# Recurrent steps of an encoder layer: turning the keys by transposing matmuls

## The chip, the cores and the metric

The kernel runs on one core of one Trainium2 chip. The metric is device time in microseconds (us), the median of several runs; less is better. Engines are named as in the profile: PE is TensorE's matmul side, PEld its weight loads, DVE is VectorE, ACT is ScalarE, POOL is GpSimd, SP is SyncE, whose queue issues the transfers.

## The reference, cut to what matters

One encoder layer with two branches, for a sequence of 1024 tokens and one of 256. The branch that the change touches is a recurrence over tokens, run forward and backward, for 16 heads of width 64:

```python
def step(S, inp):
    r_t, w_t, kh_t, ak_t, v_t, kt_t = inp
    sk = jnp.einsum('bhvk,bhk->bhv', S, kh_t)
    S = S * w_t[:, :, None, :] - sk[..., None] * ak_t[:, :, None, :] + v_t[..., None] * kt_t[:, :, None, :]
    return S, jnp.einsum('bhvk,bhk->bhv', S, r_t)
S0 = jnp.zeros((B, H, N, N), jnp.float32)
_, o = lax.scan(step, S0, (r, w, kh, ak, v, kt), reverse=reverse)
```

The rest of the layer (projections, grouped attention, gates, output projection, a feed-forward of width 4096, layer norms) is not touched. Everything is float32.

## The kernel before, in words

The kernel is a row of stages, each with its own program for every engine and a barrier behind it. The names of PSUM and SBUF tiles carry the stage: `at_` attention, `ra_` the scaled inputs, `rg_` gates, `rc_` the recurrence (the function `state_stage`), `mg_` the merge, `tl_` the tail. The order of the work on each engine is written out by hand; engines meet by semaphores.

`state_stage` does the recurrence in chunks of 64 tokens (`CH`): 40 steps `g`, 20 chunks for each of two groups of heads. A step has 8 units `u` (four pairs of heads, forward and backward), and in each unit the two heads lie on partitions 0 to 63 and 64 to 127. For unit `u`, `ub[g % 3]` holds blocks of 64 columns: values (column 0), two blocks of keys (`CH:3*CH`), two blocks of queries (`3*CH:5*CH`), and at `5*CH:6*CH` a 64x64 identity, which is written once and stays.

Scores are made by `scores(g, q)`, q = 0 to 3, two units a call, so four matmuls a call (two units by two heads). The keys are the stationary operand (64 rows, 128 columns), and 192 columns stream by: 128 of queries, which give the scores, and the 64 of the identity, which give the keys turned round. DVE multiplies the first 128 columns by a mask into `SC` (`mask`, L1738), ACT copies the last 64 into `KT` (`transposes`, L1692), once DVE's mask of the same call is done. Both wait for the one semaphore `sc_ready`, which the last matmul of the call raises.

Within step g, PE's order is: `scores(g+1,0)`; 32x32 corner matmuls (L1629), which I call X; state times queries (L1640) with the values of the next step between (L1593); `scores(g+1,1)`; two kinds of 64x64 matmuls (L1654, L1657); corner matmuls L1665; `scores(g+1,2)`; the matmuls of `Bs` by `NF` (L1601), which I call U; `scores(g+1,3)`; the state update with `KT` (L1601), K; the outputs (L1601), C. A float32 matmul stands in the trace as two weight loads and two matmul records; a transposing one, as those of the gate stage (L1165), as one of each.

SP's queue loads the units of step g+3 one at a time, each released by a point in PE's program.

Of the kernel before, what the change touches and what calls it, by code (L numbers as in the profile page):

```python
# [17 lines left out]
CH = 64  # L18
# [1456 lines left out]
def state_stage(nc, hbm, cst, pv, oR, ring, ahead, pool, ub_ready, xT, oa_ready, late):  # L1475

    with Stage(nc, "rc") as st:
# [11 lines left out]
        ps = st.psum()  # L1489
        BB, UB, OB, CB = 0, 1, 2, 3  # L1490
        ALTERNATE = (0, 4, 1, 5, 2, 6, 3, 7)
        ident64, centre = cst[:, C_ID64:C_ID64 + CH], cst[:, C_CEN:C_CEN + CH]
# [78 lines left out]
        def _(pe):  # L1571
            def scores(g, q):

                x = ub[g % 3]
                if q == 0:
                    pe.wait_ge(ub_ready[g % 3], 16 * U * (g // 3 + 1))
                    if g == 2:
                        pe.wait_ge(id_done, 1)
                n = 4 * g + q
                if n >= 2:  # L1580
                    pe.wait_ge(masked, n - 1)
                    pe.wait_ge(kt_done, n - 1)
                for j in range(2):
                    for h in range(2):
                        rows = slice(64 * h, 64 * h + 64)
                        last = pe.matmul(ps[:, 4 + 2 * (q % 2) + h, 192 * j:192 * j + 192], x[rows, 2 * q + j, CH:3 * CH],  # L1586
                                         x[rows, 2 * q + j, 3 * CH:6 * CH], start=True, stop=True)
                last.then_inc(sc_ready, 1)

            def values(g, u):  # L1590
# [14 lines left out]
            def half(h):  # L1605
                return slice(64 * h, 64 * h + 64)

            def other(h):
                return slice(64 - 64 * h, 128 - 64 * h)

            pe.wait_ge(set_up, 1)
            for q in range(4):
                scores(0, q)
            for u in range(U):
                values(0, u)
            for g in range(NSTEP):
                x, sc, v = ub[g % 3], SC[g % 2], X[g % 2]
                if g + 1 < NSTEP:
                    scores(g + 1, 0)
# [5 lines left out]
                for u in ALTERNATE:  # L1625
                    for h in range(2):
                        d = u // 4
                        i, o = (64 * h, 64 * h + 32) if d == 0 else (64 * h + 32, 64 * h)
                        last = pe.matmul(ps[o:o + 32, CB, 32 * u:32 * u + 32], sc[i:i + 32, u, h, o % 64:o % 64 + 32],  # L1629
                                         r_[d][i:i + 32, u % 4, :], start=True, stop=True)  # L1630
# [7 lines left out]
                for u in range(U):  # L1638
                    for h in range(2):
                        last = pe.matmul(ps[half(h), BB, CH * u:CH * u + CH], x[half(h), u, 3 * CH:4 * CH], S[half(h), u, :],  # L1640
                                         start=u == 0, stop=True, skip_group_check=True)
# [4 lines left out]
                if g + 1 < NSTEP:  # L1646
                    scores(g + 1, 1)
# [4 lines left out]
                for u in range(U):  # L1652
                    for h in range(2):
                        pe.matmul(ps[half(h), OB, CH * u:CH * u + CH], S[half(h), u, :], x[half(h), u, 4 * CH:5 * CH],  # L1654
                                  start=u == 0, stop=True, skip_group_check=True)
                    for h in range(2):
                        last = pe.matmul(ps[half(h), BB, CH * u:CH * u + CH], sc[other(h), u, h, 0:CH], v[other(h), u, h, :],  # L1657
                                         start=False, stop=True, skip_group_check=True)
                last.then_inc(b_ready, 1)
                pe.wait_ge(w_done, g + 1)  # L1660
                for u in ALTERNATE:
                    for h in range(2):
                        d = u // 4
                        i, o = (64 * h + 32, 64 * h) if d == 0 else (64 * h, 64 * h + 32)
                        last = pe.matmul(ps[o:o + 32, CB, 256 + 32 * u:256 + 32 * u + 32], Wt[i:i + 32, u, :],  # L1665
                                         n_[d][i:i + 32, u % 4, :], start=True, stop=True)
# [1245 lines left out]
```

## Time and profile before

| | |
|---|---|
| time, median of 3 runs | 3261.92 us (3259.46 to 3267.58) |
| the profiled execution's own time | 3262.58 us |
| its span, first to last instruction | 3260.4 us |
| PE busy | 3132.7 us, 96% of the span |
| DVE, ACT, POOL busy | 59%, 32%, 12% |
| PE and PEld records | 26248 each |
| granted TensorE clock, mean | 0.990 of full |

Busy shares are means over stages. A wait is put down to what came last by the profile; "issue" is idle time in which the engine waited for nothing that the profile shows.

### The profile page before, as it was taken

How to read it: one execution, taken by the hardware profiler on the slowest of the kernel's cores; microseconds unless marked ns; L12 is line 12 of the kernel's file. 1: busy time of each engine (PE TensorE's matmuls, PEld its weight loads, DVE VectorE, ACT ScalarE, POOL GpSimd, SP SyncE). 2: the span in 40 equal slices, each digit the busy share in tenths (PEclk: the TensorE clock that was granted, in tenths of full speed). 3: DMA queues.
4: the chain of work that ended last, by engine and by line, in shares of the span. 5: the costliest groups of instructions: out<-in, count | busy, mean ns of one | idle time of the engine just before them, and what ended most of it. 6: DMA issues, size and time to landing. Idle time of an engine off the chain costs nothing. (4 is left out here: it accounts for less than half of the span.)

```text
span 3260.4 us, 61273 instructions
## 1 busy us (share of the span) xinstructions
PE 3132.7 (96%) x26248; PEld 2098.7 (64%) x26248; DVE 1919.9 (59%) x3037; ACT 1055.9 (32%) x1731; POOL 387.1 (12%) x250
## 2 busy tenths in 40 slices
PE   9999999999999988989999999999999999999997
PEld 4565665545555556777787777667666666666665
DVE  2337762667776699546566565645555456545446
ACT  2327662334333225533443441003311111221111
POOL 0000000000000363300000233324200000300002
PEclk9999999999999999999999999999999999999998
DMA  3222101334453512455565423312122122122121
GB/s 142 58 55 53 46 32 51 118 125 141 153 173 123 209 65 90 160 180 163 165 173 153 173 92 126 140 65 72 59 65 79 63 65 78 59 97 83 60 65 65
DMA packets 225979, 336.98 MB, mean 103 GB/s; under 512 B 56112, under 2 KB 184496, under 8 KB 218672
## 3 DMA queue, kind: packets, MB, share of 16 engines
q1 hardware_dynamic: 225712, 333.08, 31.6%
q8 instruction: 209, 3.42, 0.4%
q14 instruction: 58, 0.48, 0.0%
HBM read 230.13 MB, written 96.34 MB: 100 GB/s over the span
## 5 line engine op out<-in xcount | busy, mean ns | idle before, releaser
L656 PE MATMUL ra_ps<-xT,ring 128*128 128x512 f32 (+1 forms) x1152 | 429.8, 526 | 0.0
L2415 PE MATMUL tl_ps<-merged,pool 128*128 128x320 f32 x1440 | 405.7, 434 | 2.7 <-PEq L108 2.1
L2415 PEld LDWEIGHTS tl_ps<-merged,pool 128*128 128x128 f32 x1440 | 273.9, 191 | 119.2 <-issue 5.2
L656 PEld LDWEIGHTS ra_ps<-xT,ring 128*128 128x128 f32 x1152 | 214.3, 190 | 199.0 <-issue 189.3
L2678 DVE TENSOR_TENSOR oR<-tl_ps,oR 128x320 f32<-128x320 f32 x416 | 202.0, 489 | 151.2 <-PE tl_ps L2415 148.5
L2500 ACT ACTIVATE ring<-tl_ps 128x320 f32<-128x320 f32 x96 | 42.0, 437 | 533.8 <-PE tl_ps L2415 533.8
L2415 PE MATMUL tl_ps<-hold,pool 128*128 128x320 f32 x720 | 202.6, 432 | 0.0
L2684 DVE TENSOR_TENSOR merged<-tl_ps,ring 128x320 f32<-128x320 f32 x96 | 47.2, 491 | 255.5 <-PE tl_ps L2415 140.4
L2415 PE MATMUL tl_ps<-xT,pool 128*128 128x320 f32 x640 | 182.7, 432 | 0.0
L2415 PEld LDWEIGHTS tl_ps<-hold,pool 128*128 128x128 f32 x720 | 136.8, 190 | 57.0
L2415 PE MATMUL tl_ps<-merged,sums 128*128 128x320 f32 x544 | 160.7, 435 | 5.8 <-DVE oR L2676 3.2
L317 PE MATMUL at_ps<-xT,ring 128*128 128x512 f32 (+1 forms) x432 | 159.1, 521 | 0.0
L1586 PE MATMUL rc_ps<-pool 64*128 64x192 f32 x1280 | 151.3, 354 | 7.2 <-DVE rc_ps L1787 3.9
L2415 PEld LDWEIGHTS tl_ps<-xT,pool 128*128 128x128 f32 x640 | 121.6, 190 | 50.7
L1738 DVE TENSOR_TENSOR rc_SC<-rc_ps,cst 128x512 f32<-128x512 f32 x160 | 110.2, 689 | 71.9 <-PE rc_ps L1586 71.9
L342 PE MATMUL at_ps<-at_qk 128*128 128x512 f32 (+1 forms) x288 | 129.1, 585 | 8.8 <-ACT at_p L410 8.3
L2415 PEld LDWEIGHTS tl_ps<-merged,sums 128*128 128x128 f32 x544 | 102.0, 190 | 53.8 <-issue 12.9
L354 PE MATMUL at_ps<-at_turned,at_v 32*128 32x256 f32 x2176 | 129.5, 381 | 4.5 <-DVE at_ot L494 4.1
L354 PEld LDWEIGHTS at_ps<-at_turned,at_v 32*128 32x128 f32 x2176 | 111.3, 185 | 32.4 <-issue 26.4
L317 PEld LDWEIGHTS at_ps<-xT,ring 128*128 128x128 f32 x432 | 82.1, 190 | 72.6 <-issue 68.9
L471 DVE TENSOR_REDUCE at_mx<-at_ps 128x1 f32<-128x1024 f32 (+1 forms) x80 | 84.2, 1052 | 60.8 <-PE at_ps L342 60.7
L2415 PE MATMUL tl_ps<-hold,sums 128*128 128x320 f32 x432 | 119.2, 432 | 0.0
(334 smaller groups left out, 5454.7 us busy)
## 6 DMA issues: line engine op xcount, KB each, us to landing
pool<-ub SPq DMA_DIRECT2D x320, 160.0 KB, 2.8
ub<-ra_ub SPq DMA_DIRECT2D x32, 1280.0 KB, 5.4
pool<-in_w_ff SPq DMA_DIRECT2D x32, 1024.0 KB, 4.8
pool<-in_w_ff SPq DMA_DIRECT2D x64, 512.0 KB, 3.5
ring<-in_w_in SPq DMA_DIRECT2D x38, 512.0 KB, 3.7
pool<-in_w_merge SPq DMA_DIRECT2D x15, 1024.0 KB, 4.9
ub<-ra_v SPq DMA_DIRECT2D x16, 640.0 KB, 6.4
xT<-in_xT SPq DMA_DIRECT2D x15, 640.0 KB, 6.9
```

Of the source, the lines that this page charges most:

```text
L317: last = pe.matmul(ps[:, z_bank(i) + j, 0:n], w[:, i % 3, 128 * k:128 * k + 128], xT[:, k, t0:t0 + n], start=(k == 0), stop=(k == KT - 1))
L342: last = pe.matmul(ps[:, 2 * (t % 2) + b // 512, 0:n], qk[:, h, t0:t0 + 128], qk[:, QH + h // (QH // KVH), k0 + b:k0 + b + n], start=True, ...
L354: last = pe.matmul(ps[:, 4 + i, 0:256], values_of(g, i, j), pT[g % 2][32 * i:32 * i + 32, j].rearrange("p t q -> p (t q)"), start=(j == 0) ...
L471: dve.reduce_max(mx[:, c:c + 1], scores_of(t), AX.X).then_inc(mx_done, 1)
L656: last = pe.matmul(ps[:, bank + j, 0:n], w[c][:, 128 * i:128 * i + 128], xT[:, i, t0:t0 + n], start=(i == 0), stop=(i == KT - 1))
L1586: last = pe.matmul(ps[:, 4 + 2 * (q % 2) + h, 192 * j:192 * j + 192], x[rows, 2 * q + j, CH:3 * CH], x[rows, 2 * q + j, 3 * CH:6 * CH], st ...
L1738: dve.tensor_tensor(SC[g % 2][:, 2 * q:2 * q + 2, :, :], score_view(ps, q, 0, 2 * CH), cst[:, at:at + 128].unsqueeze(1).unsqueeze(1).broad ...
L2415: last = pe.matmul(bank(n, b), lhs(k), rhs(k), start=(fresh and k == 0), stop=(k == d - 1), skip_group_check=True)
L2500: act.activation(cp[n % 2][:, c, :], bank(n, b), ACT.Copy).then_inc(done, 1)
L2678: dve.tensor_tensor(y, bank(n, b), y, ALU.add).then_inc(done, 1)
L2684: dve.tensor_tensor(hidden(n, i, j), bank(n, b), cp[n % 2][:, c, :], ALU.add).then_inc(done, 1)
```

## The change

The identity columns leave the matmuls of the scores. Each call of `scores` now first makes the scores of its four pairs of unit and head with 128 streamed columns, and then turns the keys of the same four by `pe.transpose`: keys as the stationary operand again, and the constant identity `ident64` streamed, into the PSUM columns where the turned keys stood before. `sc_ready` is raised by the last transposing matmul. What DVE and ACT do is the same, and the identity is still written into `ub`.

```diff
                 for j in range(2):
                     for h in range(2):
                         rows = slice(64 * h, 64 * h + 64)
-                        last = pe.matmul(ps[:, 4 + 2 * (q % 2) + h, 192 * j:192 * j + 192], x[rows, 2 * q + j, CH:3 * CH],
-                                         x[rows, 2 * q + j, 3 * CH:6 * CH], start=True, stop=True)
+                        pe.matmul(ps[:, 4 + 2 * (q % 2) + h, 192 * j:192 * j + 128], x[rows, 2 * q + j, CH:3 * CH],
+                                  x[rows, 2 * q + j, 3 * CH:5 * CH], start=True, stop=True)
+                for j in range(2):
+                    for h in range(2):
+                        rows = slice(64 * h, 64 * h + 64)
+                        last = pe.transpose(ps[:, 4 + 2 * (q % 2) + h, 192 * j + 128:192 * j + 192], x[rows, 2 * q + j, CH:3 * CH],
+                                            ident64[rows])
                 last.then_inc(sc_ready, 1)
```

On PE, from the corner matmuls L1665 of one step to the corner matmuls L1629 of the next, the order before is this (line, output and inputs, size, count):

```order
L1665 MATMUL rc_ps<-rc_nb,rc_Wt 32x32 x16
L1586 MATMUL rc_ps<-pool 128x192 x4
L1601 MATMUL rc_ps<-rc_Bs,rc_NF 64x64 x16
L1586 MATMUL rc_ps<-pool 128x192 x4
L1601 MATMUL rc_ps<-rc_X,rc_KT 64x64 x16
L1601 MATMUL rc_ps<-rc_SC,rc_X 64x64 x16
L1586 MATMUL rc_ps<-pool 128x192 x4
```

In the changed kernel the same stretch of PE's program (its lines are five further down) is this:

```order
L1670 MATMUL rc_ps<-rc_nb,rc_Wt 32x32 x16
L1586 MATMUL rc_ps<-pool 128x128 x4
L1591 MATMUL rc_ps<-cst,pool 128x64 x4
L1606 MATMUL rc_ps<-rc_Bs,rc_NF 64x64 x16
L1586 MATMUL rc_ps<-pool 128x128 x4
L1591 MATMUL rc_ps<-cst,pool 128x64 x4
L1606 MATMUL rc_ps<-rc_X,rc_KT 64x64 x16
L1606 MATMUL rc_ps<-rc_SC,rc_X 64x64 x16
L1586 MATMUL rc_ps<-pool 128x128 x4
L1591 MATMUL rc_ps<-cst,pool 128x64 x4
```

Nothing has moved; behind every call's four matmuls, now a third narrower, stand four more. The rows of the other engines stand as they did.

## Rows read from the trace of the kernel before

**Rows 1.** The page: transfers of instructions by queue (packets, MB, share of 16 engines).

```profile
q8 instruction: 209, 3.42, 0.4%
```

**Rows 2.** Groups of the recurrence, 1408 to 1840 us (count | busy us, mean ns | idle before).

```profile
L1586 PE MATMUL rc_ps<-pool 64*128 64x192 f32 x1268 | 149.6, 353 | 3.4 <-issue 3.3
L1738 DVE TENSOR_TENSOR rc_SC<-rc_ps,cst 128x512 f32<-128x512 f32 x159 | 109.5, 689 | 71.1 <-PE rc_ps L1586 71.1
L1692 ACT ACTIVATE rc_KT<-rc_ps 128x256 f32<-128x256 f32 x160 | 61.3, 383 | 148.9 <-DVE rc_SC L1738 148.9
...
L1697 ACT ACTIVATE rc_X<-rc_ps 64x512 f32<-64x512 f32 x80 | 47.0, 588 | 6.8 <-PE rc_ps L1593 5.2
...
L1801 DVE TENSOR_SCALAR rc_X<-rc_ps 64x512 f32<-64x512 f32 x40 | 27.8, 695 | 26.1 <-PE rc_ps L1601 26.1
L1772 DVE TENSOR_TENSOR rc_S<-rc_t,pv 128x256 f32<-128x256 f32 x72 | 27.4, 421 | 1.2
L1765 DVE TENSOR_TENSOR rc_t<-rc_ps,rc_S 128x512 f32<-128x512 f32 x36 | 24.9, 691 | 15.2 <-PE rc_ps L1601 15.2
...
L1716 ACT ACTIVATE rc_Bs<-rc_ps 128x512 f32<-128x512 f32 x40 | 23.9, 597 | 14.6 <-PE rc_ps L1657 14.4
...
L1747 DVE TENSOR_SCALAR rc_NF<-rc_nb,cst 128x128 f32<-128x128 f32 x80 | 18.9, 277 | 0.3 <-DMA rc_rb<-rb 0.3
...
L1785 DVE TENSOR_TENSOR oR<-rc_ps,oR 128x256 f32<-128x256 f32 x40 | 15.0, 416 | 0.7 <-PE rc_ps L1601 0.7
```

**Rows 3.** Busy time of the whole recurrence (window, PE, PEld, DVE, ACT, POOL, clock, DMA).

```profile
1407.90:1839.50 431.60, 394.59 (x12672) 336.47 (x12672) 256.38 (x559) 168.41 (x360) 0.17 (x1) 0.99 0.56 158
```

**Rows 4.** Timeline of 1500 to 1504.3 us (start, length, engine, line).

```profile
1500.07 0.63 PEld L1586 LDWEIGHTS rc_ps<-pool 64*128 64x128 f32 x8
1500.07 0.92 PE L1586 MATMUL rc_ps<-pool 64*128 64x192 f32 x8
...
1500.92 1.01 PEld L1601 LDWEIGHTS rc_ps<-rc_X,rc_KT 128*64 128x64 f32 x32 [0.23 <-DVE rc_X L1801]
...
1502.94 0.63 PEld L1586 LDWEIGHTS rc_ps<-pool 64*128 64x128 f32 x8
...
1503.79 0.34 PEld L1629 LDWEIGHTS rc_ps<-rc_rb,rc_SC 32*32 32x32 f32 x32 [0.23 <-issue]
```

**Rows 5.** Timeline of transposing matmuls in the gate stage, in two windows.

```profile
1361.61 0.72 PE L1165 MATMUL rg_ps<-cst,rg_inv 80*128 80x80 f32 x8
...
1300.17 0.98 PE L1165 MATMUL rg_ps<-cst,rg_inv 120*128 120x120 f32 x8
```

**Rows 6.** Timeline of 1507.8 to 1513.1 us.

```profile
1508.22 0.63 PEld L1586 LDWEIGHTS rc_ps<-pool 64*128 64x128 f32 x8
...
1508.37 0.61 DVE L1755 SCALAR_TENSOR_TENSOR rc_NF<-rc_nb,cst,rc_ps 128x128 f32<-128x128 f32 x2 [0.81 <-PE rc_ps L1665]
1509.09 0.34 PEld L1601 LDWEIGHTS rc_ps<-rc_Bs,rc_NF 64*64 64x64 f32 x8 [0.25 <-issue]
...
1510.53 0.78 PEld L1601 LDWEIGHTS rc_ps<-rc_Bs,rc_NF 64*64 64x64 f32 x24 [1.10 <-issue]
```

**Rows 7.** Waits of PE in the recurrence (line, total us, times, longest).

```profile
PE rc_ps L1665 <- issue: 11.7, 8, 2.0
PE rc_ps L1657 <- issue: 7.6, 8, 1.6
...
PE rc_ps L1593 <- issue: 0.8, 1, 0.8
```

**Rows 8.** Windows from the end of one such wait to the end of the next.

```profile
1505.62:1510.53 4.91, 3.94 (x126) 3.16 (x126) 1.99 (x4) 2.60 (x6) 0.00 (x0) 1.00 0.66 188
...
1548.33:1553.14 4.81, 2.90 (x127) 2.43 (x127) 0.69 (x1) 2.16 (x4) 0.00 (x0) 1.00 0.58 159
```

**Rows 9.** Transfers of instructions in the recurrence, 1407.9 to 1839.5 us.

```profile
q8 instruction: 100, 1.64, 1.6%
```

**Rows 10.** Two windows of the gate stage, before and in transposing matmuls.

```profile
1207.00:1218.70 11.70, 4.35 (x17) 2.73 (x15) 11.15 (x18) 1.67 (x4) 1.47 (x1) 0.80 0.36 120
1218.90:1220.20 1.30, 1.30 (x8) 1.30 (x9) 1.30 (x1) 0.37 (x1) 0.00 (x0) 0.50 0.04 13
```

## The prediction

> **What bounds the kernel now.** I read the page first. The change touches one stage, so the next view is the busy time of that stage alone: 431.6 us for 40 steps, 10.8 us a step, with PE busy for 394.6 us and DVE and ACT for 256.4 and 168.4 [rows 3]. PE is the engine to look at, and the reader is to see that it still lacks 37 us. The list of its waits says where: almost all of it is "issue", idle time that no semaphore explains. There are seven such lines with 38 waits and 33.3 us together (11.7 for the first, 0.8 for the last), single ones up to 2.0 us [rows 7]. PE's last matmul runs on for some 0.2 us when the queue is already dry, so PE's program stood still for about 33.3 + 38 x 0.2 = 41 us.
>
> The timeline shows such a wait in the middle of one row of like matmuls: 8 weight loads of U from 1509.09, then nothing for 1.10 us, then the other 24 [rows 6]. Counting between the ends of two such waits gives the cause. From 1505.62 to 1510.53 there are 126 loads and 126 matmuls, and from 1548.33 to 1553.14 there are 127 of each, with quite different work inside [rows 8]: a fixed number of instructions, about 253. The transfers of instructions tell the same. The page has 209 on the queue q8 with 3.42 MB [rows 1], 16.4 KB each, which over 2 x 26248 records is 65 bytes a record; the recurrence has 100 of them [rows 9] for 2 x 12672 records [rows 3], one per 253. So PE's program arrives in pieces of some 253 records, a piece is used up in 4.3 us on average (431.6 / 100), and 38 times in 100 the next one is late. In this stage PE is bound partly by its work and partly by the arrival of its program.
>
> **The change, part by part.** A call before is 8 matmul records in 4 pairs, the two heads of a pair side by side. Its first load starts at 1500.07 and the loads of the next work at 1500.92, 0.85 us later; the same from 1502.94 to 1503.79 [rows 4]. Its matmuls span 0.92 us, and the records are at least 0.32 us long, so with a first load of some 0.11 the four pairs follow at (0.92 - 0.32 - 0.11) / 3 = 0.16 us, for 192 columns.
>
> *Removed: 64 of 192 columns.* A third of 0.16 is 0.054, for four pairs 0.215 us a call. The weight load of 128 columns then has 0.11 us to hide in instead of 0.16; the stage's loads do that now for the 64-column forms (32 loads in 1.01 us, 0.06 a pair, row of 1500.92 in [rows 4]), and I take 0.11 for a pair.
>
> *Added: four transposing matmuls, one record each.* The gate stage has such records at 80 columns, 8 in 0.72 us, and at 120, 8 in 0.98 [rows 5]. With lengths of about 0.23 and 0.27 for the last, they follow at 0.070 and 0.102 us, about 0.8 ns a column; 64 columns are 0.055. All those span 80 or 120 rows, and none shows two halves of the array side by side. Bounds: two by two, 0.11 us a call; one behind the other, 0.22. The regular halves run side by side, so I take the first. A call then gives back 0.215 - 0.11 = 0.10 us of PE, 16 us over 160 calls; by the upper bound, nothing.
> The Trainium skill, "TensorE: Matmul & The Clock Gate", section Terms, has a transpose mode that is four times faster for FP32. By it the 64 columns would cost a quarter of 0.107, 0.03 a pair, and PE's saving would be 0.16 a call and 25 us in all; the gate stage's records, at twice that time, speak against it, and the sum goes by them.
>
> *What of it reaches the end.* Two of the four calls of a step have a cover. After `scores(g+1,2)`, U needs `NF`, which DVE has at 1508.37 + 0.61 = 1508.98, when the call has just run out (loads until 1508.85) and U starts at 1509.09 [rows 6]. After `scores(g+1,3)`, K waits for DVE's L1801 (the mark on the row of 1500.92 [rows 4]). Shorter calls there lengthen those waits. That leaves two calls, 0.2 us a step, 8 us at most. A second loop bounds it further: from U's end L1801 (0.70), K (1.01), L1765 (0.69), L1772 twice (27.4 / 36 = 0.76), the outputs twice (0.75), L1747 twice (0.47), the mask L1738 (0.69), ACT's L1692 (0.38), L1697 twice (1.18), L1692 again (0.38), L1716 (0.60) and U itself (about 0.95) are 8.6 us [rows 2, 4], and twelve handovers of 0.03 to 0.2 us make it 9.3 or more. A step without its share of the 41 us is (431.6 - 41) / 40 = 9.8 with the ends of the stage in it. The loop holds one mask of a first call, so 0.1 a step at most comes through it. I take -1 us, between 0 and -8, near the loop's end of it.
>
> *Added: records.* A call has 8 loads and 8 matmuls now and will have 8 + 4 of each: 8 records more, 1280 in 160 calls, 5.05% of 25344, five pieces more. The time from one piece to the next when PE waits is set by the transfer, not by what PE did; what changes is the work that a piece holds. Work is 431.6 - 41 = 390.6 us, 3.91 us a piece, then 390.6 / 105 = 3.72. Each late piece is met 0.19 us earlier. 38 waits become 38 x 1.05 = 40 and their mean goes from 1.08 to 1.27: 50.8 us against 41, +10. Of the 62 pieces that were in time, those less than 0.19 us ahead become late. Lateness runs over 2 us for 38 pieces, some 19 per us, and it is denser near zero; with the 62 spread over one us, 12 become late by 0.1: +1. A saving of work also comes back 40% as waiting. And the five more joints have their share of bad luck, up to 5 x 4.3 = 21.5 us if no piece had slack. I take +13 for all of it, somewhat over the bare +11.
>
> **Sum:** -1 + 13 = +12 us on the profiled execution's 3262.6, 3274.6. The median of the runs is 0.7 below that execution, so 3274. A measurement can tell about 0.3%, 10 us.
>
> **Rivals.** (a) *The arrival of the program sets the whole pace.* Then 105 pieces at 4.3 us: +21 us, 3284. For it: 38 waits in 100, and the time from piece to piece where PE waited is 4.91 and 4.81 us [rows 8], longer than the mean. Against it: 62 pieces without a wait. (b) *The shorter calls make up for it.* All 8 us of the uncovered calls arrive while waits grow by 10: -4 to +5, 3263. It needs DVE's and ACT's loop to be slacker than its sum. (c) *Faster.* The masks wait for calls, 71.1 us in all [rows 2], and each call ends 0.10 us earlier, so the loop shortens at all four calls: 0.4 a step, -16 us, against which the pieces are late less than thought, because they are asked for earlier too; it decides if the growth of the waits stays under 6 us. 3252. The Trainium skill, "Perfetto Trace Analysis", section Transposes, asks for a transpose instead of a standard matmul wherever one is logically meant; that speaks for this side, and no run here shows it yet. (d) *Transposing costs more than its columns.* One behind the other, with a gap for the change of mode, or a lower clock: clock 0.50 stands over eight transposing matmuls of the gate stage [rows 10]. But PE had been busy for only 4.35 of the 11.7 us before, and at 1300.17 the same form runs at the full rate [rows 5]. With 0.1 us more a call +16 on top, 3290. The Trainium skill, "TensorE: Matmul & The Clock Gate", Part 4, says that transpose mode does not count as PE being busy for the clock; the gate stage doesn't settle it, as PE was idle there anyway.
>
> **How the numbers follow.** The forecast, +6 to +18 us: 0.55. (a) 0.13, (b) 0.20, (c) 0.06, (d) 0.06. The range of eight in ten leaves out the lower edge with (c) and the upper with (d): 3260 to 3288. The forecast's own range is 3268 to 3281. Slower by over 0.3%: three quarters of the forecast with (a) and (d), 0.41 + 0.13 + 0.06 = 0.60. Within 0.3%: the rest of the forecast and (b), 0.34. Faster: 0.06.
>
> **What the profile of the changed kernel would show.** The queue q8 has 214 packets, 105 in the recurrence. PE has 26888 records. A call's loads and matmuls reach the next work in 0.75 us instead of 0.85; if it is still 0.85, the transposing records ran one behind the other. Busy time of PE in the stage falls by up to 16 us while its "issue" waits grow from 33 to 45 us or more, in some 50 places. The waits of U and K for DVE grow by about 0.1 us each. I am wrong if the issue waits don't grow (the pieces then were not what PE waited for), or if the stage gets shorter than 425 us.

## The result, and the profile after

The changed kernel takes 3288.07 us (median of 4 runs, 3285.79 to 3289.22), the kernel before 3264.75 us (4 runs). The ratio is 1.0069, 95% interval 1.0055 to 1.0083: slower by 22.5 us, between 18 and 27. The forecast was slower by 12 us, 3274; 12 lies below the interval.

The profiled execution has a span of 3284.9 us, 24.5 more than before. The page's row for the transfers of instructions answers to [rows 1]: five more on q8.

```profile
PE 3140.4 (96%) x26888; PEld 2123.3 (65%) x26888; DVE 1919.3 (58%) x3037; ACT 1057.1 (32%) x1731; POOL 387.0 (12%) x250
...
q8 instruction: 214, 3.51, 0.5%
```

PE has 26888 matmul records, 640 more, and as many more loads. Windows of the changed kernel, in the recurrence and behind it (window, PE, PEld, DVE, ACT, POOL, clock, DMA), beside [rows 3]:

```profile
1409.10:1861.40 452.30, 396.46 (x13312) 358.33 (x13312) 256.18 (x556) 169.16 (x360) 0.10 (x1) 0.96 0.54 151
1861.40:3284.90 1423.50, 1388.78 (x5102) 969.18 (x5100) 779.00 (x1406) 300.34 (x542) 243.12 (x149) 0.99 0.25 84
```

For the kernel before, a window set to the recurrence alone and one to what follows it:

```profile
1408.00:1838.70 430.70, 394.55 (x12672) 336.45 (x12672) 255.67 (x556) 168.41 (x360) 0.07 (x1) 0.99 0.56 159
1838.70:3260.40 1421.70, 1386.94 (x5102) 967.98 (x5100) 778.18 (x1406) 300.23 (x542) 242.97 (x149) 0.99 0.25 84
```

The recurrence grew by 452.3 - 430.7 = 21.6 us, what follows by 1.8, and what stands ahead by 1.1. DVE and ACT did the same work in it to within 1 us.

One call in the timeline of the changed kernel answers to [rows 4]:

```profile
1506.84 0.52 PEld L1586 LDWEIGHTS rc_ps<-pool 64*128 64x128 f32 x8
1506.84 0.71 PE L1586 MATMUL rc_ps<-pool 64*128 64x128 f32 x8
...
1507.28 0.25 PEld L1591 LDWEIGHTS rc_ps<-cst,pool 64*128 64x128 f32 x4
1507.39 0.28 PE L1591 MATMUL rc_ps<-cst,pool 64*128 64x64 f32 x4
...
1507.60 0.34 PEld L1634 LDWEIGHTS rc_ps<-rc_rb,rc_SC 32*32 32x32 f32 x32
```

From the first load at 1506.84 to the loads of the corner matmuls at 1507.60 it is 0.76 us, against 0.85 before. The transposing matmuls cost what was forecast: four take 0.28 us with a last one of 0.22, so the two pairs follow at 0.06, and the two halves of the array work side by side. The change thus spares PE 0.09 us a call, some 14 us over 160 calls. None of it reaches the end, and PE's busy time in the stage didn't fall either: it is 396.5 us after 394.6. PE's waits for its program answer to [rows 7]; these are the largest of the kind in the recurrence:

```profile
PE rc_ps L1670 <- issue: 18.1, 13, 2.0
PE rc_ps L1606 <- issue: 10.8, 15, 1.4
PE rc_ps L1659 <- issue: 10.0, 11, 1.4
PE rc_ps L1662 <- issue: 5.3, 7, 1.3
```

With five smaller lines (11 waits, 5.4 us) they are 57 waits with 49.6 us now, 38 with 33.3 before. With 0.2 us each for the matmul that still ran, PE's program stood still for 61 us instead of 41: +20, nearly the whole 21.6. The distance between the ends of such waits is again nearly the same number of records, 128 matmuls and 128 loads here for one piece, and 251 and 252 for two (beside [rows 8]):

```profile
1588.79:1593.01 4.22, 3.22 (x128) 2.89 (x128) 1.35 (x4) 1.45 (x4) 0.00 (x0) 1.00 0.65 180
...
1513.14:1521.78 8.64, 8.28 (x251) 7.48 (x252) 6.30 (x14) 2.98 (x7) 0.00 (x0) 1.00 0.49 138
```

And q8 brought 105 pieces during the recurrence, where [rows 9] has 100:

```profile
q8 instruction: 105, 1.72, 1.7%
```

The packet times in the two traces tie the waits to these transfers directly. Before the change the start of PE's next matmul or load comes over 0.6 us behind the last one 35 times in the recurrence, and 34 of these gaps end 1.1 to 1.7 us after a transfer on q8 has landed; after the change 50 of 52 do. The transfers start 4.23 us apart on average before and 4.22 after, and don't overlap: each takes 1.1 us, and the next starts 2.3 us or more after its end.

### The profile page after: what moved, and what is told of

Read it like the earlier page. It is cut to its first block and busy times, and to the rows that moved or that the text cites. A ratio compares the mean times of both kernels' runs of the same rounds, so it can differ in the third digit from the quotient of the medians.

```text
span 3284.9 us, 62553 instructions
## 1 busy us (share of the span) xinstructions
PE 3140.4 (96%) x26888; PEld 2123.3 (65%) x26888; DVE 1919.3 (58%) x3037; ACT 1057.1 (32%) x1731; POOL 387.0 (12%) x250
## 5 line engine op out<-in xcount | busy, mean ns | idle before, releaser
L1586 PE MATMUL rc_ps<-pool 64*128 64x128 f32 x1280 | 119.4, 306 | 4.5 <-DVE rc_ps L1792 3.9
```

The lines of the kernel that those rows point to most:

```text
L1586: pe.matmul(ps[:, 4 + 2 * (q % 2) + h, 192 * j:192 * j + 128], x[rows, 2 * q + j, CH:3 * CH], x[rows, 2 * q + j, 3 * CH:5 * CH], start=Tru ...
```

## The experiments

Theory A is that of the prediction: the recurrence pays for the pieces in which PE's program arrives, so for records, whatever they do. Theory B is that the transposing matmuls, or PE's work, set the time. Theory A follows the size of the measured loss, so its ranges are mostly higher than the +13 of the forecast. All times are against the kernel before on the same chip; a ratio is turned into us by 3263.

**Records alone.** Eight of the sixteen corner matmuls of a step are made twice, which gives the change's number of records without touching the scores.

```diff
-                for u in ALTERNATE:
+                for u in (*ALTERNATE[:4], *ALTERNATE):
                     for h in range(2):
                         d = u // 4
```

> The kernel before, with 8 of the 16 corner matmuls L1629 of each step made twice (the first result is overwritten by the same one), so 32 more records a step, as many as the change adds, and no transposing matmul. The 64 records of this line take 0.38 us a step, so 32 more are some 0.19 us of PE, 7.6 us over 40 steps. Theory A, the arrival of the program: 105 pieces instead of 100, waits for it grow as in the changed kernel, the time +18 to +28 us. Theory B, the transposing matmuls themselves (their clock or their place) cost the time: +0 to +8 us.

Measured: ratio 1.0053 (1.0035 to 1.0070), +17 us (11 to 23). The recurrence has the change's records:

```profile
1406.80:1855.50 448.70, 403.04 (x13312) 344.68 (x13312) 255.87 (x557) 169.34 (x360) 0.15 (x1) 0.99 0.53 153
```

Most of the loss is there without one transposing matmul, and it is well over this kernel's 8 us of added work. The value is just under theory A's range, and its interval reaches into it.

**Twice as many.** The same with all sixteen (`(*ALTERNATE, *ALTERNATE)`).

> The kernel before with all 16 corner matmuls L1629 of each step made twice, 64 more records a step and 0.38 us more of PE, 15 us in all. Theory A: 110 pieces at 4.3 us or a little less, twice the loss of the run with 8, +36 to +50 us. Theory B: no more than the work, +0 to +15 us.

Measured: ratio 1.0089 (1.0066 to 1.0112), +29 us (22 to 37). The recurrence took 467.1 us for 110 pieces, in an execution 9 us above the median. The loss is more than the work, so theory B falls here too, but it is less than twice the loss with eight, and below the range I gave theory A but for the end of its interval.

**Narrow scores, nothing turned.** No record is added, and some 34 us of PE's work, by the estimate of the prediction, are taken away. DVE sets the PSUM banks to zero once, ahead of the steps; `KT` is zero and the state lacks its updates.

```diff
-                        last = pe.matmul(ps[:, 4 + 2 * (q % 2) + h, 192 * j:192 * j + 192], x[rows, 2 * q + j, CH:3 * CH],
-                                         x[rows, 2 * q + j, 3 * CH:6 * CH], start=True, stop=True)
+                        last = pe.matmul(ps[:, 4 + 2 * (q % 2) + h, 192 * j:192 * j + 128], x[rows, 2 * q + j, CH:3 * CH],
+                                         x[rows, 2 * q + j, 3 * CH:5 * CH], start=True, stop=True)
```

> The kernel before with 128 streamed columns instead of 192 in the scores and no turning of keys at all: ACT copies zeros into KT, so the state is not updated by them. Records stay as they are, PE's work falls by 0.215 us a call, 34 us in all. If the loop through DVE and ACT and the arrival of the program bound the stage (theory A), little of it arrives: 0 to -8 us, with issue waits that grow. If PE's own work bounds it (theory B): -20 to -34 us.

Measured: ratio 1.0000 (0.9988 to 1.0012), nothing, within 4 us. The profiled execution's recurrence is 6 us shorter:

```profile
1410.00:1834.80 424.80, 373.02 (x12672) 327.33 (x12672) 256.11 (x557) 166.93 (x360) 0.00 (x0) 0.97 0.55 160
```

This is the sharpest of the runs. A third of the scores' streaming is worth at most a few us. PE's busy time fell by 21.5 us and not by 34; the granted clock of 0.97 and 12 more waits, each with the end of a matmul that counts as busy, account for part of the difference. PE's waits for the program grew from 33.3 to 37.8 us, in 50 places. Zeroing the banks costs about 2 us once: at the start of the stage PE waits 6.0 us for DVE instead of 3.9. PE is busy for 394.6 of 431.6 us in [rows 3], and still its work isn't the bound.

**Both together.** Narrow scores, nothing turned, and eight corner matmuls twice: the change's records with less work than the change.

> The kernel before with 128 streamed columns and no turning of keys (ACT copies zeros into KT), and 8 of the 16 corner matmuls L1629 made twice: the changed kernel's number of records and its narrow scores, without one transposing matmul. PE's work is 34 us less than before, plus 7.6 us for the doubled matmuls. Theory A, a price per record through the arrival of the program, about 0.018 us each in the runs so far: +17 to +24 us, as the changed kernel. Theory B, transposing matmuls cost part of it: clearly less, +0 to +12 us.

Measured: ratio 1.0073 (1.0058 to 1.0088), +24 us (19 to 29), the change's own loss, at the upper end of theory A's range and over all of theory B's.

```profile
1408.90:1859.60 450.70, 383.20 (x13312) 337.36 (x13312) 256.03 (x557) 168.52 (x360) 0.00 (x0) 0.97 0.53 151
```

No transposing matmul is in this kernel. What separates it from the narrow one is 32 records a step, with an estimated 7.6 us of work in all.

**Records taken away.** Half of the output matmuls of each step are left out, in the kernel before and in the changed one; part of the outputs is missing.

```diff
-                heads(ps, OB, lambda u, h: v[:, u, h, :], lambda u, h: sc[:, u, h, CH:2 * CH], False).then_inc(o_ready, 1)
+                heads(ps, OB, lambda u, h: v[:, u, h, :], lambda u, h: sc[:, u, h, CH:2 * CH], False, (1, 3, 5, 7)).then_inc(o_ready, 1)
```

> The kernel before with 8 of the 16 output matmuls C left out in each step (odd units; part of the outputs is missing), 32 records fewer a step. PE's work falls by 0.23 us a step, 9 us in all, as much as 32 records always carry. Theory A: 95 pieces, the time falls by 15 to 22 us. Theory B: by no more than the work, 0 to -9 us.

> The changed kernel with the same 8 output matmuls of each step left out (part of the outputs is missing), so it has as many records as the kernel before. Theory A: within 4 us of the kernel before, and 17 to 24 us above the run with these matmuls left out of the kernel before. Theory B: still 14 us or more above the kernel before.

Measured: without them the kernel before is at 0.9948 (0.9932 to 0.9965), -17 us (-22 to -11). The changed kernel without them is at 0.9994 (0.9983 to 1.0004), -2 us, in effect the kernel before, whose number of records it has:

```profile
1407.30:1835.30 428.00, 377.69 (x12672) 339.71 (x12672) 255.76 (x556) 166.00 (x360) 0.13 (x1) 0.96 0.55 160
```

Each is in theory A's range; the two lie 15 us apart, where theory A had 17 to 24. Theory B's +14 is excluded.

**Where it ends.** Fourteen of the sixteen left out (`(7,)` in place of `(1, 3, 5, 7)`), 91 pieces.

> The kernel before with 14 of the 16 output matmuls C of each step left out (most of the outputs is missing), 56 records fewer a step, 91 pieces instead of 100. PE's work falls by 0.4 us a step, 16 us in all. Theory A with 4.3 us for every piece: -35 to -38 us. Theory A with a second bound, the loop through DVE and ACT of 9.3 us a step: less than in proportion to the run with 8 left out, -20 to -32 us. Theory B: -5 to -16 us, its work.

Measured: ratio 0.9938 (0.9921 to 0.9954), -20 us (-26 to -15). Taking away 24 records a step more than in the run before gave 3 us more, and the intervals overlap. With 4.3 us for every piece it should have been -35 to -38; with a second bound I had expected -20 to -32, and the value is at the near end of that.

```profile
1407.20:1810.90 403.70, 364.77 (x11552) 306.25 (x11552) 255.33 (x556) 164.38 (x360) 0.10 (x1) 0.98 0.59 169
```

So at about 10 us a step something besides the program holds PE up. Its waits say what, in part:

```profile
PE rc_ps L1640 <- DVE rc_S L1772: 12.6, 36, 1.1
```

Before, this wait was there once, with 0.3 us. PE now waits 36 times for DVE's L1772 to finish the state, while 23.9 us of waits for the program are left. L1772 is a member of the prediction's loop through DVE and ACT, which it put at 9.3 us or more; that the rest of this loop is what makes L1772 late was argued, not shown.

**Half of the change.** The change in two of the four calls, once where DVE's work covers the calls and once where it doesn't (`if q >= 2:` and `if q < 2:` around the new form, the old one in the `else`).

> The change made in the calls 2 and 3 of each step alone, whose shorter time is hidden behind DVE's L1755 and L1801. 16 records more a step, 102 to 103 pieces. Theory A: half of the change's loss, +8 to +13 us. Theory B, the shorter calls matter and only covered ones are lost: more than half of the loss, +14 us or more, here, and about none in the calls 0 and 1.

> The change made in the calls 0 and 1 of each step alone, which no wait for DVE follows, so that 0.1 us of each can arrive, 8 us at most. 16 records more a step. Theory A with the loop as the bound: +8 to +13 us, as in the calls 2 and 3. If saved PE time arrives here: 0 to +5 us.

Measured: covered calls 1.0026 (1.0016 to 1.0037), +8.5 us; uncovered 1.0017 (1.0007 to 1.0027), +5.5 us. Each has 103 pieces. Half of the records give somewhat less than half of the loss. The covered calls are in theory A's range. The uncovered ones miss it, and are close to what I had expected if saved time arrives there; whether they let some of their 0.09 us through stays open, as the intervals of the two overlap (5 to 12 us and 2 to 9).

**Traffic.** The kernel before with four more loads a step into a tile that nobody reads; PE's program is unchanged. This is the first of the four:

```diff
+                    after(sp, dumped[0], 16 * g)
+                    load_unit(sp, hbm, dump, g + 3, 0, dumped[0])
```

> The kernel before with half as much traffic again in the recurrence: the loads of the units 0, 2, 4 and 6 are each followed by another of the same size into a tile that nobody reads. PE's program is the same. If the price of a piece of program lies partly in its transfer standing behind the data's (share of the transfer engines 0.56 now), the pieces take longer and the stage grows by 0.2 us or more a piece, +15 to +50 us. If it is a fixed delay of the fetch: within 5 us.

Measured: ratio 1.0046 (1.0031 to 1.0061), +15 us (10 to 20), in the range for pieces that stand behind data, at its lower end.

```profile
1411.80:1854.90 443.10, 397.76 (x12672) 338.42 (x12672) 256.07 (x557) 168.38 (x360) 0.19 (x1) 0.99 0.70 209
```

It has the same records as in [rows 3] and nearly the same busy times, traffic of 209 GB/s instead of 158, and 12.4 us more than the 430.7 for the same 100 pieces, 0.12 us each. The packet times agree: a piece's own transfer takes 1.1 us as before, but the time from its end to the start of the next grew from 3.12 to 3.25 us. That fits pieces that queue with the data. That the units' own loads came late instead was not excluded by a run, though PE has no wait for a transfer in the recurrence, before or here.

**Two variants for their own sake.** The first turns the keys of both heads of a unit by one transposing matmul over all 128 rows: 20 records a call. Against the changed kernel, with the new places in PSUM and what reads them left out here:

```diff
                 for j in range(2):
-                    for h in range(2):
-                        rows = slice(64 * h, 64 * h + 64)
-                        last = pe.transpose(ps[:, 4 + 2 * (q % 2) + h, 192 * j + 128:192 * j + 192], x[rows, 2 * q + j, CH:3 * CH],
-                                            ident64[rows])
+                    last = pe.transpose(ps[:, 4 + 2 * (q % 2) + j, 256:384], x[:, 2 * q + j, CH:3 * CH], cst[:, C_ID:C_ID + 128])
```

> The changed kernel, but the keys of both heads of a unit are turned by one transposing matmul over all 128 rows, two a call instead of four. Records: 20 a call, against 16 before and 24 in the change, so 102 to 103 pieces. PE's work in a call grows, since the array goes from halves to the whole. Theory A, a price per record: +8 to +12 us against before, half of the change's loss. Theory B, the transposing form costs: as the change, +18 us or more.

Measured: ratio 1.0037 (1.0023 to 1.0050), +12 us (8 to 16), as theory A had it. It is better than the change and worse than before. The call costs PE more:

```profile
1505.77 0.52 PEld L1586 LDWEIGHTS rc_ps<-pool 64*128 64x128 f32 x8
...
1506.41 0.20 PEld L1589 LDWEIGHTS rc_ps<-cst,pool 128*128 128x128 f32 x2
...
1506.78 0.34 PEld L1631 LDWEIGHTS rc_ps<-rc_rb,rc_SC 32*32 32x32 f32 x32 [0.17 <-issue]
```

That is 1.01 us, 0.16 more than before, 26 us in all; PE's busy time in the recurrence is 418 us, 23 more. Yet the recurrence took only 439.2 us, 8.5 more, and PE's waits for its program shrank to 19.0 us in 33 places. Most of the added work went into time that PE had stood still before. So the waits alone don't measure the price: what grew with the 103 pieces is the time for all of them, 4.26 us each.

The second keeps the kernel before and moves the loads of the attention outputs behind those of the units (`range(8 * (g - 36), 8 * (g - 36) + 8) if g >= 36` in place of one at each g from 2 to 33).

> The kernel before, with the 32 loads of attention outputs (160 KB each) moved from the steps 2 to 33 to the last four steps, where the units' loads have ended. Half as much traffic again cost 15 us, so a tenth less in 32 steps would give back about 3 us by the arrival of the program: -1 to -5 us. It could lose where the merge then waits for these loads: up to +10 us.

Measured: ratio 1.0010 (1.0000 to 1.0021), +3 us (0 to 7). The recurrence took 429.3 us in the profiled execution, against 430.7. The expected gain of 1 to 5 us didn't come: moving this traffic, a tenth of the whole by the expectation, to the end brought nothing. No run with more than half of the outputs computed beat the kernel before.

## Why the prediction was right, and where its size was off

**The bound.** "In this stage PE is bound partly by its work and partly by the arrival of its program" named the right mechanism with too much weight on the work. The narrow run takes a third of the scores' streaming away and gains nothing that can be told. The profiled executions side by side show how little the work counts (times in us, of the recurrence):

| kernel | pieces | PE busy, per piece | recurrence, per piece |
|---|---|---|---|
| before | 100 | 3.95 | 4.31 |
| the change | 105 | 3.78 | 4.31 |
| eight corner matmuls twice | 105 | 3.84 | 4.27 |
| sixteen twice | 110 | 3.77 | 4.25 |
| narrow scores | 100 | 3.73 | 4.25 |
| narrow scores, eight twice | 105 | 3.65 | 4.29 |
| half of the outputs | 95 | 3.99 | 4.34 |
| the change, half of the outputs | 100 | 3.78 | 4.28 |
| the change in the covered calls | 103 | 3.84 | 4.29 |
| the change in the uncovered calls | 103 | 3.80 | 4.23 |
| 128-row transposing matmuls | 103 | 4.06 | 4.26 |
| attention outputs loaded late | 100 | 3.95 | 4.29 |
| an eighth of the outputs | 91 | 4.01 | 4.44 |
| more traffic | 100 | 3.98 | 4.43 |

PE's busy time per piece varies by 11%. The time per piece varies by under 3%, but for the two last: one has the other wait, and one has the added traffic. What sets these 4.3 us, of which a transfer itself takes 1.1, stays open.

**The price of the transposing form.** Forecast 0.10 us a call given back, records side by side at 0.055 us; measured 0.09 and 0.06. The estimate by the Trainium skill, "TensorE: Matmul & The Clock Gate", section Terms, 0.03 a pair, is off by a factor of two. Rival (d), a higher cost or a lower clock, fell as the cause of the loss. The transposing matmuls run side by side. The granted clock did fall, from 0.99 in the recurrence to 0.96 (the engine was at the lower of its two levels, 1.2 GHz, for some 32 us of it instead of 10), but it is 0.96 as well in the changed kernel with half of its outputs, which is as fast as before, and 0.99 in the run with eight matmuls doubled, which lost 17 us. By my estimate the lower clock is also why PE's busy time didn't fall by the forecast "up to 16 us": 22 us more at half the rate are some 11 us of work done later, and 19 more waits leave some 4 us of matmuls that run on, which together make up for the 14 that the calls give back.

**What of it reaches the end.** Forecast -1 us between 0 and -8. The narrow run has twice the saving per call and 0 us (within 4), in agreement. With it rivals (b) and (c) fell, which both needed the saved time to arrive; so did the advice that (c) leans on, in this kernel, where the identity columns cost no record of their own. One sign missed: the waits of U and K for DVE were to grow by 0.1 us each, and they didn't. The loads of K wait for DVE's `X` 35 times with 6.5 us, after 37 times with 9.3 before. Why is not shown.

**The added records.** Five pieces more, 214 on q8 and 105 in the stage, came as forecast. The step that was mis-sized is "I take +13 for all of it": the term measured 20 us in waits and 21.6 in the stage. The working held the time of a piece fixed, made work per piece 0.19 us less, and let only the 38 late pieces and 12 more feel it. Instead 57 places waited, 19 more, with the mean about as before (61 / 57 = 1.07 us against 1.08). I took the 62 pieces without a wait for pieces with slack of their own. The table speaks against that: the time per piece hardly moves when the work in it does, so what PE gains on one piece it waits for at a later one, and five pieces more cost nearly their whole time. The prediction had this case in hand, as "up to 5 x 4.3 = 21.5 us if no piece had slack", and didn't take it. Rival (a), which it gave 0.13, has the mechanism that the table bears out and the right size: +21 us, with 4.31 us a piece before and after. As a rule for the medians of all runs it is an upper price. From 95 pieces (-17 us) over 100 to 110 (+29 us) it is 46 us for 15, 3.1 us a piece, or 12 ns for each of its 253 records.

**The range** of 3260 to 3288 has the median of 3288.07 at its upper edge, and the forecast's own range, 3268 to 3281, doesn't hold it. That the outer range reached so far owes much to rivals (a) and (d), and (d) fell. The direction was forecast rightly: the chances put 0.60 on slower by over 0.3%.

## What to carry to other kernels

Where PE runs many small float32 matmuls, count records before columns: here an estimated 0.2 us of streaming less per call bought nothing, and eight records more a call cost 23 us. The sign to look for is "issue" idle in the middle of a run of like matmuls, at a fixed distance in records (here 253, one transfer on the instruction queue). A change that splits a matmul to make its parts cheaper should be priced by the transfers of instructions that it adds, each at up to the stage's time per transfer.

## What the runs showed of the hardware

A transposing float32 matmul is one load and one matmul record where a regular one is two of each: the change's 640 transposing matmuls added 640 of each. At 64 rows, two of them run side by side on the two halves of the array: 64 columns in 0.06 us a pair, with loads of 138 ns at the median where regular ones of 128 columns have 188. More data traffic alone lengthened a stage whose program arrives during it: 158 to 209 GB/s, 15 us. PE's waits for its program end 1.1 to 1.7 us after a transfer on the instruction queue has landed, in 34 of 35 cases before the change and 50 of 52 after it. The granted clock in the recurrence was 0.96 to 0.98 in the seven kernels with narrower scores in some or all calls, and 0.98 or 0.99 in the others; the lower clock came without a loss that could be told in two of them (the narrow run, and the changed kernel with half of its outputs).
